# The last head of a gated-delta mixer: its norm statistics split in two, its output squared and gated out of PSUM

## The reference

```python
q = l2_normalize(conv_q) * 128 ** -0.5         # per head
k = l2_normalize(conv_k)
o, S = gated_delta_rule(q, k, v, g, beta, S0)  # recurrence over chunks of the prompt; one step for new tokens
o = rms_norm(o, o_norm) * silu(z)              # o * rsqrt(mean(o * o) + EPS) * o_norm * silu(z)
y = o.reshape(B, T, 8 * 128) @ w_out
```

## Time and profile before

| | |
|---|---|
| median of three runs | 1487.43 us |
| the three runs | 1487.43, 1489.12, 1486.07 us |
| the profiled execution, its own time | 1479.54 us |
| span of the profile | 1477.6 us |
| mean granted TensorE clock | 0.988 |
| busy: PE, DVE, ACT, POOL | 94%, 46%, 34%, 25% |

### The profile page before, as it was taken

One profiled execution on the slowest core, in us unless ns is written; L12 is line 12 of the kernel. 1 busy time (PEld: TensorE's weight loads), 2 busy tenths in 40 slices (PEclk: granted clock), 3 DMA queues, 4 the chain that ended last, 5 costly groups with the idle time before them and its releaser, 6 DMA issues.

```text
span 1477.6 us, 28241 instructions
## 1 busy us (share of the span) xinstructions
PE 1382.8 (94%) x11788; PEld 1163.3 (79%) x11788; DVE 684.6 (46%) x976; ACT 499.2 (34%) x707; POOL 376.4 (25%) x471
## 2 busy tenths in 40 slices
PE   6998889999999999898999999998799999999996
PEld 4765478888888888777787788787688888888885
DVE  5345534333333332676775775775443333333222
ACT  5233434322323231334344344344233223233231
POOL 2003411222222010542443443444021212221010
PEclk9999999999999999989999999999999999999999
DMA  7355603333233322010121120120222232323311
GB/s 277 150 200 172 208 29 108 118 115 114 87 111 118 118 79 85 29 58 30 58 77 40 58 86 30 58 86 16 80 100 93 86 114 85 113 96 118 118 39 59
DMA packets 31325, 140.92 MB, mean 95 GB/s; under 512 B 4457, under 2 KB 6761, under 8 KB 18954
## 3 DMA queue, kind: packets, MB, share of 16 engines
q1 hardware_dynamic: 31242, 139.75, 27.0%
HBM read 128.63 MB, written 11.11 MB: 95 GB/s over the span
## 4 chain that ended last, share of the span: by engine, by line
PE 83%; DVE 12%; issue 2%; ACT 2%; DMA 0%; POOL 0%; DVEq 0%; SPq 0%; ACTq 0%; POOLq 0%
PE P L1570 59%; PE P L1927 8%; PE P L1918 7%; DVE arena L1337 2%; PE P L1933 2%; DVE arena L1378 1%; DVE wl L1059 1%; DVE arena L1492 1%; PE P L2092 1%; PE P L2082 1%; ACT wh L727 1%; PE P L1665 1%; PE P L2053 1%; PE P L1902 1%; PE P L1770 1%
## 5 line engine op out<-in xcount | busy, mean ns | idle before, releaser
L1570 PE MATMUL P<-zh,wh 128*128 128x260 f16 x1728 | 334.1, 275 | 17.3 <-DVE wl L1059 13.4
L1570 PE MATMUL P<-zl,wh 128*128 128x260 f16 x1728 | 334.0, 275 | 0.0
L1570 PE MATMUL P<-zh,wl 128*128 128x260 f16 x1728 | 333.8, 274 | 0.0
L1570 PE MATMUL P<-arena,wh 128*128 128x260 f16 x1920 | 292.5, 274 | 7.3 <-DVE arena L1189 3.2
L1059 DVE SCALAR_TENSOR_TENSOR wl<-stage,wh 128x2048 f16<-128x2048 f32 (+1 forms) x77 | 189.5, 2460 | 224.5 <-ACT wh L693 196.0
L1570 PEld LDWEIGHTS P<-arena,wh 128*128 128x128 f16 x1920 | 185.8, 97 | 38.3 <-issue 5.8
L1570 PEld LDWEIGHTS P<-zh,wh 128*128 128x128 f16 x1728 | 166.6, 97 | 50.0 <-issue 23.2
L1570 PEld LDWEIGHTS P<-zh,wl 128*128 128x128 f16 x1728 | 167.9, 97 | 26.9
L1570 PEld LDWEIGHTS P<-zl,wh 128*128 128x128 f16 x1728 | 167.7, 97 | 26.8
L1570 PE MATMUL P<-arena,wl 128*128 128x260 f16 x960 | 184.7, 274 | 0.0
L693 ACT ACTIVATE wh<-stage 128x2048 f16<-128x2048 f32 (+1 forms) x82 | 165.6, 2019 | 2.9 <-PE P L1918 2.9
(11 more groups left out here) (317 smaller groups left out, 1513.1 us busy)
## 6 DMA issues: line engine op xcount, KB each, us to landing
stage<-w_gu SPq DMA_DIRECT2D x44, 1024.0 KB, 4.8
stage<-w_in SPq DMA_DIRECT2D x24, 1024.0 KB, 4.9
stage<-w_dn SPq DMA_DIRECT2D x16, 1408.0 KB, 6.0
arena<-cache_k SPq DMA_DIRECT2D x32, 256.0 KB, 3.3
stage<-w_out SPq DMA_DIRECT2D x8, 1024.0 KB, 6.4
arena<-cache_v SPq DMA_DIRECT2D x32, 256.0 KB, 2.9
arena<-delta_state SPq DMA_DIRECT2D x8, 512.0 KB, 3.7
o_ds<-arena SPq DMA_DIRECT2D x8, 512.0 KB, 6.8
```

The costliest lines, as they stand in the source:

```text
L1570: mm = nc.tensor.matmul(pm[j][:, c, :], w[:, wslot, o:o + 128], x[:, k, c * CH:(c + 1) * CH], start=(k == first and w is wh and x is xh), ...
```

## The change

1. POOL, head 7: `square_q` multiplies the square of q by EPS * 128 * 128 in a second pass in place. `gate_out` and `gate_lo` of head 7 are gone from POOL.
2. TensorE, head 7, chunk 2: `stat_query` puts q's term into `stat` and leaves the accumulation open.
3. ACT, head 7: no copy of the output. The 8 columns of new tokens are squared ahead; the 512 of the prompt are squared straight from bank 7.
4. TensorE: block 0 of the second tile moves ahead of the statistics; `stat_last` adds the squares to the open accumulation.
5. DVE: `add_query` and `head_scale` of head 7 are gone. It gates the output from bank 7 (o * o_norm * silu(z)) once the squares are made, multiplies by the factor once that is there, and forms the low half itself.

```diff
@@ square_q (POOL)
-                nc.gpsimd.tensor_tensor(qq[h % 2], x, x, MUL).then_inc(nqq, 1)
+                if h == HG - 1:
+                    link(nc.gpsimd.tensor_tensor(qq[h % 2], x, x, MUL))
+                    nc.gpsimd.tensor_scalar(qq[h % 2], qq[h % 2], EPS * 128 * 128, None, MUL).then_inc(nqq, 1)
+                else:
+                    nc.gpsimd.tensor_tensor(qq[h % 2], x, x, MUL).then_inc(nqq, 1)
@@ end of the mixer (POOL)
-            gate_out(HG - 1)
-            gate_lo(HG - 1)
             sum_squares(3)
@@ end of the loop over heads (ACT)
-                act.wait_ge(*G("o_ps", h + 1))
-                if h >= 2:
-                    act.wait_ge(yo, h - 1)
-                nc.scalar.activation(oh1[:, h % 2, 0:SEQ], P[:, 7, :], ACT.Copy).then_inc(S["o"], 1)
-                head_square(h)
+                if p < HG:
+                    act.wait_ge(*G("o_ps", h + 1))
+                    if h >= 2:
+                        act.wait_ge(yo, h - 1)
+                    nc.scalar.activation(oh1[:, h % 2, 0:SEQ], P[:, 7, :], ACT.Copy).then_inc(S["o"], 1)
+                    head_square(h)
+                else:
+                    act.wait_ge(du, HG)
+                    act.wait_ge(o1stat, HG - 1)
+                    nc.scalar.activation(ssq[:, SEQ:], oh1[:, h % 2, SEQ:], ACT.Square)
+                    act.wait_ge(*G("o_ps", h + 1))
+                    nc.scalar.activation(ssq[:, 0:SEQ], P[:, 7, :], ACT.Square).then_inc(o1sq, 1)
             head_factor(HG - 1)
             head_hi(HG - 1)
@@ behind the loop over heads (DVE)
-            add_query(HG - 1)
-            head_scale(HG - 1)
+            z, o = sz[:, (HG - 1) % 2, :], oh1[:, (HG - 1) % 2, :]
+            w = par[:, P_ONORM:P_ONORM + 1]
+            dve.wait_ge(zsilu, HG)
+            dve.wait_ge(o1sq, HG)
+            nc.vector.scalar_tensor_tensor(out=o[:, 0:SEQ], in0=P[:, 7, :], scalar=w, in1=z[:, 0:SEQ],
+                                           op0=MUL, op1=MUL)
+            link(nc.vector.scalar_tensor_tensor(out=o[:, SEQ:], in0=o[:, SEQ:], scalar=w, in1=z[:, SEQ:],
+                                                op0=MUL, op1=MUL))
+            dve.wait_ge(o1rs, HG)
+            dve.wait_ge(m1_lo, HG - 1)
+            nc.vector.tensor_tensor(yn1, o, ors1, MUL).then_inc(yz, 1)
+            dve.wait_ge(yz, HG)
+            dve.wait_ge(m1_hi, HG)
+            nc.vector.tensor_tensor(ml1[:, HG - 1, :], yn1, mh1[:, HG - 1, :], SUB).then_inc(m1_lo, 1)
@@ phase_in_two (TensorE)
+                pe.wait_ge(*G("s", 4 * HG))
+                pe.wait_ge(pm_free, t)
+                product(1, 0, 128, xh, xl, KD, 256, range(1), ready)
                 mid()
-                pe.wait_ge(pm_free, t)
-                product(1, 0, 128, xh, xl, KD, 256, range(early), ready)
+                product(1, 0, 128, xh, xl, KD, 256, range(1, early), ready)
@@ new (TensorE)
+            def stat_query():
+                pe.wait_ge(nqq, HG)
+                ready(HG - 1, "w")
+                pe.wait_ge(*G("u", 4 * (HG - 1) + 1))
+                for c in range(2):
+                    nc.tensor.matmul(stat[:, c, :], onesH[:, :], qq[(HG - 1) % 2][:, c * CH:(c + 1) * CH],
+                                     start=True, stop=False)
+
+            def stat_last():
+                pe.wait_ge(o1sq, HG)
+                for c in range(2):
+                    mm = nc.tensor.matmul(stat[:, c, :], onesH[:, :], ssq[:, c * CH:(c + 1) * CH],
+                                          start=False, stop=True)
+                mm.then_inc(o1stat, 1)
@@ the four chunks (TensorE)
                     elif c == 2 and h + 1 < HG:
                         stat_l2(h + 1)
+                    elif c == 2:
+                        stat_query()
@@ behind the loop over heads (TensorE): stat_last takes the place of out1_mid
-            def out1_mid():
-                pe.wait_ge(*G("s", 4 * HG))
-                stat_head(HG - 1)
```

More of the change, by code:

```diff
@@ L2098, in _ @@
                 fill(4)
-            def out1_mid():
-                pe.wait_ge(*G("s", 4 * HG))
-                stat_head(HG - 1)
-            phase_in_two("out1", mh1, ml1, HG - 1, len(OUT1_CALLS), out1_mid, lambda k: pe.wait_ge(m1_lo, k + 1))
+            phase_in_two("out1", mh1, ml1, HG - 1, len(OUT1_CALLS), stat_last, lambda k: pe.wait_ge(m1_lo, k + 1))
             phase("gu1", zh, zl, z_ready(3), lambda: statistics(3))
```

## The result

| | before | after |
|---|---|---|
| median, first comparison (5 runs each) | 1486.78 us | 1478.81 us (1476.29 to 1479.83) |
| profiled execution, its own time | 1479.54 us | 1478.98 us |
| span of the profile | 1477.6 us | 1477.0 us |
| mean granted TensorE clock | 0.988 | 0.988 |

The profiled executions differ by 0.6 us only. One timed run of the kernel before, of 2060.91 us at a granted clock of 0.651, was in a slower state and is left out of all numbers here. So two questions stand: what the change does in its own place, and where the other numbers come from. The first view is the chain of waits of the changed kernel over the last head; it answers to the earlier trace rows. L2120 is what was L2082, L1968 is `stat_query`, L1974 `stat_last`, L1591 a block.

The account below looks back on a forecast made before the run. TensorE, busy 94%, bounds the kernel; its queue and the last head's chain end together. Of 4.12 us lost, 0.22 stays: 3.9 won, less 0.47 for stat_query, is 3.4 off 1487.43, giving 1484.0 us, range 1481.8 to 1487.0.

Parts of the forecast that it names:

- the same 3.4 off the median: Whole kernel: the 3.4 us won in the last head was subtracted from the three-run median 1487.43, giving 1484.0.
- stat_query costs 0.47: Head 7, chunk 2 on TensorE: four added matmuls lengthen the path by 0.47 us, the rest hidden beside DVE's subtraction.
- A standing still of 0.22: TensorE before block 0 and the statistics in the last head: standing still shrinks from 2.17 to 0.22 us.
- The prediction's own sign of being wrong: Last head: a pause over 0.5 before the statistics, clock of 0.50, wait before block 7, or L1448 moving with POOL.
- Block 0 takes 0.69: TensorE, second tile, ahead of the statistics: block 0 runs from 1065.91 to 1066.60.
- Statistics 0.88, clock at 1.00, blocks without a gap: TensorE, last head: no clock fall, statistics take 0.88 instead of 2.02 us, blocks 1 to 6 follow in 4.03.
- Square from PSUM 0.61, DVE passes 0.77: Last head's chain: ACT's square from PSUM takes 0.61 us, DVE's factor product and low half 0.77 each.
- POOL's second pass costs nothing: POOL, square_q of head 7: the extra pass takes 1.53 us, normalize_k(7) moves some 0.6 later, cost 0.
- Rival E: Head 7 at 1015 to 1021: POOL's second pass delays normalize_k(7), making the kernel slower, 1490.9 at 11 us; chance 0.05 with everything slower.
- B: Last head: the clock's fall is absent in timed runs before, so gain is 2.3 us, 1485.1; chance 0.27.
- C: Last head: the clock falls after the change too, ahead of the statistics; gain 1.5 us, 1485.9; chance 0.06.
- D: Last head: a DVE split held by POOL's pass or a longer hand-over chain eats 0.5; gain 2.9 us, 1484.5; chance 0.10.

Follow-up runs that it names:

- e2: The changed kernel again, unchanged, timed in the same rounds as the kernel before: ratio 0.998 (0.9965 to 0.9996).
- e12: The changed kernel a third time, unchanged, against the kernel before: ratio 0.9971 (0.9954 to 0.9987), median 1481.48 us.
- e7: Changed kernel with stat_query's two matmul pairs split over chunks 1 and 2 and block 0's long-met waits moved ahead; against the kernel before 0.997, stretch 11.92 us.
- e1: The kernel before, unchanged, timed beside itself: ratio 0.9999 (0.9985 to 1.0013).
- e8: Kernel before with only q's term ahead (POOL's second pass, stat_query, stat_last, no add_query): ratio 1.0004, stretch 15.26 us.
- e9: Kernel before with only the last head's gate and low half moved from POOL to DVE: ratio 0.999, stretch 15.50 us.
- e3: Kernel before with only block 0 of the second tile issued ahead of the statistics: ratio 0.9987, stretch 14.85 us.
- e10: Kernel before with eight unused matmuls filling the pause ahead of the last head's statistics: ratio 0.9996, stretch 14.79 us.
- e5: Changed kernel with 20 unused matmuls ahead of TensorE's wait at the second mixer's start; against the kernel before 0.9971, median 1479.26 us.
- e6: Changed kernel with 20 unused matmuls at the second mixer's start and further groups in the first mixer; against the kernel before 0.9985.
- e4: Changed kernel with block 0 put back behind the statistics; against the kernel before 0.9994, stretch 12.90 us.

## Why the prediction was right or wrong

The sign was right, the time outside the range: 1478.81 against 1484.0, 1481.8 to 1487.0. The step that failed is the one that took the same 3.4 off the median: "The median of the three runs, 1487.43, is 7.9 above the profiled time, for which the trace has no explanation".

The three runs, "from 1.4 below to 1.7 above their median", were taken as the scatter of this kernel. They are not. Over three later sessions the kernel before ran 102 times beside the experiments, from 1479.32 to 1488.10, in clusters that go with the mean clock: near 1479.5 at 0.988, 1482.3 at 0.986 and 0.987, 1486.5 at 0.982, 1487.4 at 0.980. 46 runs were at 1486.0 or more, 11 below 1480.5. The changed kernel ran 24 times (e2, e12), from 1476.10 to 1486.35, in clusters some 3 us lower: the lowest runs of the two are 1479.32 and 1476.10, 3.22 apart. The profiled execution before was of the lowest cluster and the three runs of the upper one, and both stood in the table: 7.9 us between one execution and three others of the same program was the measure of the scatter, and the range should have reached down by as much.

In the two sessions where both kernels ran the means are 1484.72 (69 runs) and 1481.57 (24 runs); they differ by 3.15 us, with a standard error of 0.69 (2.3 in the first of the two, 4.0 in the other). The forecast of 3.4 fits that, the 8.0 of the first comparison doesn't. So the first comparison is the 3.2 of the stretch and 4.8 that e2 and e12 don't show again: all five runs of before lay in the upper clusters and all five of after in the lower ones. Why is open. Of the later runs 46 of 102 of before were at 1486.07 or more and 7 of 24 of after at 1479.83 or less; with independent draws five out of five would come about once in 50 times for the one and once in 500 for the other. So chance alone is a poor explanation and a condition of that session a likely one, but no run shows it.

By its own steps, for the stretch:

- *stat_query costs 0.47.* From one L2120 to the next it takes 1066.67 - 1064.42 = 2.25 against 1.79 in the earlier trace rows: 0.46. Right.
- *A standing still of 0.22.* It is 0.52, from the end of the output matmuls at 1068.26 to 1068.78. The path from the state update's start to block 0 takes 0.71 and was taken as the 0.41 of a chunk. Block 0 has three waits behind each other where a chunk has one, the "0.35 issue" of the chain. In e7, with two of them moved ahead, it is 0.49. An undersized term, by 0.30. What is left of the 0.49 above the 0.41 isn't explained. The prediction's own sign of being wrong, a pause of over 0.5 before the statistics, is just met if block 0's wait is counted so.
- *Block 0 takes 0.69.* It takes 0.83 until the statistics start: 0.14 too little. Against this, block 7 takes 0.68 instead of 0.86 and starts the additions 0.18 earlier than the sum had it.
- *Statistics 0.88, clock at 1.00, blocks without a gap.* 0.88, 1.00 in both windows, one piece of 42 matmuls. Right. The sum: 3.41 forecast, less 0.30 and 0.14, plus 0.18, is 3.15; measured 3.16.
- *Square from PSUM 0.61, DVE passes 0.77.* 0.60, and 0.70 for each of both passes. Block 7 is released by TensorE's own queue, with 0.23 to spare where 0.18 was forecast. Right.
- *POOL's second pass costs nothing.* The timeline of POOL after, which answers to the earlier trace rows:

```profile
1014.58 1.52 POOL L566 TENSOR_SCALAR arena<-arena 128x520 f32<-128x520 f32 x1
...
1019.00 1.28 POOL L580 TENSOR_TENSOR arena<-arena 128x520 f32<-128x520 f32 x1 [0.18 <-POOL arena L556]
```

and DVE's user of it, which was L1448:

```profile
1022.54 0.67 DVE L1457 TENSOR_TENSOR arena<-P,arena 128x512 f32<-128x512 f32 x1
```

The pass takes 1.52 (priced 1.53) and POOL's wait ahead of normalize_k shrinks from 1.05 to 0.18. Counted from chunk 1's first product of head 7, which is 2.58 later in this profile, normalize_k starts 0.80 later (forecast 0.6) and L1457 where L1448 did: 1022.54 - 2.58 = 1019.96. From the marker to chunk 2's first product of head 7 it is 1061.84 - 206.47 = 855.37 before and 1064.42 - 209.10 = 855.32 after: nothing lost. Rival E is out.

The rivals. B, no fall in the timed runs before: e1, e8 and e9 have the fall, as before has, and e3 shows a kernel nearly like it without one. Without a fall the gain is 14.79 - 12.57 = 2.2 (forecast 2.3). For the lowest cluster the runs tell: both profiles of before lie in it (1479.54 and 1479.50) and have the fall, its 12 runs, one of e1's among them, lie within 0.53 us (1479.32 to 1479.85), and a run without the fall would lie some 0.9 below (an estimate from e10), where there is none. How often the runs of the other clusters have it isn't seen; 3.15 with its error fits 2.2 and 3.2. C is out: no profile with the whole change, seven of them, has a fall in the stretch. D in its hand-over part is what cost the 0.30. Its other part, a DVE split held by POOL's pass, isn't there: the split beside L566 takes 0.76, against 0.69 in the earlier trace rows, and nothing behind it is late. But the pass moves normalize_k beside another split, and that one is held (1.55, in the last section); it costs the path nothing.

## What to carry to other kernels

Where two queues end together, read what each is worth with the other left as it is: here three of the four parts alone won 1.6 us together, and the whole 3.2. If the profiled execution and the timed ones of one kernel are far apart, the scatter is at least that distance, and the range must hold it; compare two kernels from a marker behind the part that scatters, to the end, and a few tenths can be told from two profiles. Waits that are long met cost about 0.1 us each right behind the one that matters, and less ahead of it (0.35 against 0.14 for two of them, e7). Fillers paid where TensorE was certain to wait longer than they last (e5), and in e6, where it wasn't certain, they got onto the path.

## What the runs showed of the hardware

- The granted clock differs in the first mixer between executions of one program (clock A 0.85 and 0.83 in e2 and e12, 0.92 in after), and so does the time, by up to 8.8 us of 1484 (102 runs of before); transfers that land late stand beside it in the chain, and the shares aren't separated. In the stretch it fell while TensorE stood or right behind: in before, e1 and e9 after a pause of 2.17, in e8 after one of 1.43. It didn't fall with the pause of e4, nor in e3, where block 0 lies in the pause, nor in head 7's earlier pause of 1.68.
- One split of DVE (L1371, 128x512) beside POOL's normalize_k took 1.55 us, twice its usual 0.69; it began 0.27 after that pass (1019.00 to 1020.28) and ended 0.54 after its end, without anything on the path behind it:

```profile
1014.98 0.76 DVE L1371 SCALAR_TENSOR_TENSOR wl<-stage,wh 128x512 f16<-128x512 f32 x1
...
1017.23 0.68 DVE L1371 SCALAR_TENSOR_TENSOR wl<-stage,wh 128x512 f16<-128x512 f32 x1
...
1019.27 1.55 DVE L1371 SCALAR_TENSOR_TENSOR wl<-stage,wh 128x512 f16<-128x512 f32 x1
```

The split at 1014.98, beside the pass at 1014.58, took 0.76. The Trainium skill (SBUF — State Buffer, Who interferes with whom) has the two exclude each other for a whole instruction. The split at 1019.27 comes near to that: held until 1020.28 and then 0.69 long it would end at 1020.97, and it ended at 1020.82. The one at 1014.98 doesn't: POOL's pass lasted until 1016.10, and the split was done at 1015.74. What tells the two cases apart wasn't tried.
- The same four matmuls of the statistics took 0.88 us behind other work, and 1.11 to 1.13 after a pause with the clock granted at 1.00 throughout (e3, e4), and 0.92 right behind fillers (e10).
